# Which expert matrices are converted ahead of time, how many conversions run at once, and how four tiles are gathered: a two-layer mixer and mixture-of-experts trunk on eight cores

## The reference

```python
for l in range(DEPTH):                       # 2
    m = hybrid_mixer(x, w_in[l], ..., w_o[l])
    x = layer_norm(ALPHA * x + m, ln1_g[l], ln1_b[l])
    f = grouped_moe(x, router_w, router_b, exp_w_gate[l], exp_w_up[l], exp_w_down[l])
    x = layer_norm(ALPHA * x + f, ln2_g[l], ln2_b[l])
```

```python
for e in range(N_EXPERTS):                   # 16, width 512, two of them per token
    h = jax.nn.silu(xt @ w_gate[e]) * (xt @ w_up[e])
    y = y + dense_gates[:, e:e + 1] * (h @ w_down[e])
```

## Time and profile before

| what | value |
|---|---|
| runs | 2025.96, 2028.21, 2029.23 us; median 2028.21 |
| profiled execution, its time | 2037.57 us |
| its span on the slowest core (core 2) | 2036.5 us |
| spans of the eight cores | 2007.5 to 2036.5 us |
| TensorE, VectorE, ScalarE, GpSimd busy | 62%, 51%, 31%, 24% of the span |
| first mixer, first expert stage | to about 598 us, 598 to 961 us |
| second mixer, second expert stage | 961 to 1549 us, 1549 to 1902 us |
| last gathers, norm and stores | from 1902 us |

### The profile page before, as it was taken

One profiled execution on the slowest core, in us unless ns is written; L12 is line 12 of the kernel. 1 busy time (PEld: TensorE's weight loads), 2 busy tenths in 40 slices (PEclk: granted clock), 3 DMA queues, 4 the chain that ended last, 5 costly groups with the idle time before them and its releaser, 6 DMA issues.

```text
span 2036.5 us, 23801 instructions; the slowest of 8 cores (2007.5 to 2036.5 us)
## 1 busy us (share of the span) xinstructions
PE 1260.2 (62%) x7040; PEld 640.8 (31%) x7040; DVE 1041.5 (51%) x2328; ACT 637.1 (31%) x1109; POOL 496.1 (24%) x361
## 2 busy tenths in 40 slices
PE   0577868586429698685254687767535967878200
PEld 0433333232215454342121233333223534544000
DVE  1357486757733232232279658675761322323597
ACT  0344544435202222120254254443421211211122
POOL 4011315041340000001845112303031000000597
PEclk9897879798659899897567798978766989989655
DMA  9947667759848999997965878974124999997663
GB/s 199 260 137 99 99 94 125 104 89 180 160 123 208 260 224 249 246 236 222 206 134 64 112 93 115 125 89 90 63 84 144 236 244 230 247 256 168 225 210 131
DMA packets 78766, 334.99 MB, mean 164 GB/s; under 512 B 10776, under 2 KB 22688, under 8 KB 62880
## 3 DMA queue, kind: packets, MB, share of 16 engines
q0 software_dynamic: 26384, 166.16, 50.1%
q1 hardware_dynamic: 52240, 167.14, 25.3%
HBM read 362.71 MB, written 147.19 MB: 250 GB/s over the span
## 4 chain that ended last, share of the span: by engine, by line
PE 38%; DMA 17%; DVE 16%; issue 15%; ACT 8%; POOL 3%; DVEq 0%; SPq 0%; ACTq 0%; another core or an unknown queue 0%; POOLq 0%
PE pb L596 36%; DMA yg<-s_scr 6%; DMA s_wbuf<-ew 3%; DMA s_xy<-xg 3%; DMA s_xtok<-x 2%; ACT s_scr L605 2%; PE pT L1287 1%; ACT s_xy L641 1%; DVE s_sm L624 1%; ACT L605 1%; ACT s_xtok L605 1%; DVE s_scr L609 1%; DVE s_sm L675 1%; DVE s_scr L616 1%; DVE s_xtok L609 1%
## 5 line engine op out<-in xcount | busy, mean ns | idle before, releaser
L596 PE MATMUL pb<-s_xy,s_wbuf 128*128 128x352 bf16 (+2 forms) x2992 | 657.4, 349 | 145.2 <-ACT s_scr L605 34.5
L596 PEld LDWEIGHTS pb<-s_xy,s_wbuf 128*128 128x128 bf16 x2992 | 288.6, 104 | 396.3 <-issue 237.0
L596 PE MATMUL pb<-s_wbuf,s_scrb 128*128 128x512 bf16 (+1 forms) x768 | 232.1, 399 | 51.6 <-DMA s_wbuf<-ew 28.4
L616 DVE TENSOR_SCALAR s_scr<-pb,s_gsl 128x512 f32<-128x512 f32 (+1 forms) x192 | 135.6, 745 | 234.8 <-PE pb L596 167.6
L596 PE MATMUL pb<-s_wbuf,s_xy 128*128 128x512 bf16 x792 | 239.2, 412 | 8.9 <-DVE s_xtok L624 2.2
L609 POOL TENSOR_TENSOR s_xtok<-s_xtok,s_lnp 128x1024 f32<-128x1024 f32 x76 | 183.8, 2422 | 199.8 <-ACT s_xtok L605 153.4
L609 DVE TENSOR_TENSOR s_scrb<-s_scr,pb 128x352 bf16<-128x352 f32 x128 | 64.6, 519 | 229.9 <-PE pb L596 218.8
L406 POOL DMA_DIRECT2D s_wbuf<-exp_w x42 | 22.4, 532 | 645.8 <-PE pb L596 577.8
L641 ACT COPY s_xy<-pT 128x1024 bf16<-128x1024 bf16 (+1 forms) x96 | 90.3, 940 | 283.4 <-PE pT L1287 253.2
L1287 PE MATMUL pT<-s_identb,s_xy 128*128 128x128 bf16 (+1 forms) x768 | 121.9, 226 | 89.0 <-DMA s_xy<-xg 53.2
L709 PE MATMUL pT<-s_identb,s_scr 128*128 128x128 bf16 x336 | 55.0, 273 | 182.2 <-ACT s_scr L605 70.5
(11 more groups left out here) (119 smaller groups left out, 1619.2 us busy)
## 6 DMA issues: line engine op xcount, KB each, us to landing
ew<-exp_w POOLq DMA_DIRECT2D x36, 1536.0 KB, 17.8
s_wbuf<-ew SPq DMA_DIRECT2D x54, 1024.0 KB, 14.6
s_wbuf<-exp_w POOLq DMA_DIRECT2D x42, 1024.0 KB, 15.4
yg<-s_scr SPq DMA_DIRECT2D x64, 512.0 KB, 15.0
s_xy<-xg SPq DMA_DIRECT2D x32, 514.0 KB, 13.4
yg<-s_scr SPq DMA_DIRECT2D x32, 384.0 KB, 17.8
xg<-s_gov SPq DMA_DIRECT2D x2, 5808.0 KB, 31.4
s_xtok<-x SPq DMA_DIRECT2D x17, 512.0 KB, 10.6
```

Of the source, the lines that this page charges most:

```text
L596: em.op(PE, lambda e: e.matmul(out.ap, lhsT.ap, rhs.ap, start=start, stop=stop), w=[out], r=[lhsT, rhs])
L616: em.op(E, lambda e: e.tensor_scalar(out=out.ap, in0=a.ap, scalar1=a1, scalar2=None, op0=op0), w=[out], r=rr)
```

## The change

Three things:

1. `PRE` becomes all experts but 3, 7, 11 and 15: 12 of 16 are converted ahead, four are loaded from float32. A layer has 24 conversions of experts instead of 18, and 12 converting loads instead of 21.
2. `NTOK` becomes 3, and the planner charges a conversion 4 bytes per element instead of 6 (11.65 us at 270 GB/s instead of 17.5).
3. Between the layers tiles 0 to 3 are gathered plainly into four staging places in `wbuf` from column 16384 on, the place of w_o, and added by `vt`; tiles 2 and 3 reuse the places of 0 and 1. w_o is loaded after that, at the start of the second layer's list, and no longer before the branch. Tiles 4 to 16 are gathered as before.

```diff
-PRE = [e for e in range(NE) if e % 2 == 0 or e == 1]
+PRE = [e for e in range(NE) if e % 4 != 3]
...
-NTOK = 2
+NTOK = 3
...
                 em.dma(POOL, ewD[l].ap[e, h * 64:(h + 1) * 64, :], ew_d[l, e, h * 64:(h + 1) * 64, :], "dew%d" % k,
-                       w=[ewD[l].rows(2 * e + h, 2 * e + h + 1), tok[k].rows(0, 1)], r=after, size=64 * 12288 * 6)
+                       w=[ewD[l].rows(2 * e + h, 2 * e + h + 1), tok[k].rows(0, 1)], r=after, size=64 * 12288 * 4)
...
-                   w=[wmD.rows(h, h + 1), tok[k].rows(0, 1)], r=[gtok.rows(NT - 1, NT)], size=32 * 24576 * 6)
+                   w=[wmD.rows(h, h + 1), tok[k].rows(0, 1)], r=[gtok.rows(NT - 1, NT)], size=32 * 24576 * 4)
...
             if l > 0:
+                stg = [View(wbuf, 16384 + k * 2 * D, F32, D) for k in range(4)]
+                for i in range(4):
+                    for k in range(2):
+                        c, g = k * NT + i, stg[(2 * i + k) % 4]
+                        gc = gai(2 * i + k, 2 * i + k + 1)
+                        em.gather(g().ap, ygD[l - 1].ap, gc.ap, "dg%d" % c, w=[g(), gtok.rows(i, i + 1)],
+                                  r=[ygD[l - 1].rows(0, NSLOT + 1), gc])
+                    for k in range(2):
+                        vt(xtile(i), stg[(2 * i + k) % 4](), xtile(i), ALU.add)
+                load_layer_weights(l, only=[4])
                 for (t0, nb) in MBLOCKS:
                     for k in range(2):
-                        for i in range(t0 // 128, (t0 + nb) // 128):
+                        for i in range(max(4, t0 // 128), (t0 + nb) // 128):
                             c_gather(k, i, ygD[l - 1])
...
-                load_layer_weights(l + 1)
+                load_layer_weights(l + 1, only=range(4))
```

## The result

The changed kernel takes 2099.84 us (median of four runs) where the kernel before takes 2027.39 in the same comparison: a ratio of 1.0343, 95% interval 1.0312 to 1.0375. It is 3.4% slower; 1970 was forecast, with a range up to 2008. The ratio leaves out the fourth run, 2121.36 us, in which four of the cores showed a lower granted clock (0.77 to 0.79 in place of 0.80). The profiled execution took 2100.09 us, its span 2099.0 on core 2, the slowest again.

A forecast was written before the change was run, and what follows sets the result against it. It took full DMA to bound the expert stages and chains over four engines the mixers; -52 - 9.9 + 0 - 7 + 10.2 = -58.7 us from the 2028.2 median gives 1970 us, range 1942 to 2008.

The forecast's parts named there:

- Part 1: Expert stages: three more experts a layer read as bf16 save 26 us a stage, 52 for both; bounds 13 and 31.4.
- Part 2: End of the first layer: without the output matrix's load ahead, the last store lands sooner, gaining 9.9 us; bounds 5 and 9.9.
- Part 3: Between the layers: four plainly gathered tiles change nothing, 0 us; bounds a gain of 8, a loss of 10.
- Part 4: Mixers: more conversions planned closer make GpSimd wait and cost 10.2 us; bounds 0 and 80.
- c: Mixers: the time one conversion piece takes when others are queued, 12.6 us as the mean of four bursts.
- the half of the lateness: Mixers: of 20.4 us by which the last pieces run late, half, 10.2 us, was taken to lengthen the kernel.
- the prediction's own formulas: Lateness at a mixer's last piece, piece time against planned time: 12.1 us in the first layer, 8.3 in the second.
- E: Rival, mixers: pieces take 13.9 us and all lateness passes on, losing 80 us; +11, 2040 us; decided at 13.65; chance 0.08.
- Part 5: End of the first mixer: the last conversion no longer stands among the late scatters, gaining 7 us, between 0 and 11.7.

The follow-up runs named there:

- e1: Changed kernel, but each layer converts only expert 0 and all bf16 experts read expert 0's matrices: 1963.2 us, ratio 0.965 to the kernel before.
- e9: Changed kernel with copies of expert 0's bf16 form in place of the other eleven experts' conversions: 1971.4 us, ratio 0.971 to the kernel before.
- e11: Kernel before with w_o loaded later, ten experts converted in the first layer and twelve in the second, 14.6 us a piece, three under way: 1982.9 us, ratio 0.975.
- e13: Kernel before with w_o loaded later, twelve experts converted in both layers, 14.6 us a piece, three under way, all gathers adding: 2011.2 us, ratio 0.989.
- e14: Kernel before with w_o loaded later, eleven experts converted in the first layer and twelve in the second, 14.6 us a piece, three under way: 1991.0 us, ratio 0.980.
- e2: Kernel before with only the gathers' change: four tiles gathered plainly and w_o loaded after them: 2040.4 us, ratio 1.0035.
- e6: Kernel before with only the load of w_o moved behind gathers of the second layer, all gathers adding: 2039.2 us, ratio 1.0015.
- e5: Changed kernel with the planner's price of a conversion at 14.6 us a piece in place of 11.65: 2046.4 us, ratio 1.0047 to the kernel before.
- e10: Kernel before with only the planner's price of a conversion changed, 11.65 us in place of 17.5: 2097.9 us, ratio 1.033.

## Why the prediction was wrong

**Part 1** was right in kind and too small: the second stage is 36.9 us shorter (26 taken, 31.4 the upper bound), the first 38.2, of which part 2 has about 10. In the other runs with twelve experts (e1, e9, e11, e13, e14) the second stage gains 29 to 35 us. 31.4 counted only what the three experts' own transfers save, and was no bound. The queues in the first stage, 660 to 950 us:

```profile
q1 hardware_dynamic: 15206, 61.07, 63.9%
q0 software_dynamic: 1649, 12.07, 26.3%
```

They moved 73.1 MB in 290 us, 252 GB/s, against 238 in the earlier trace rows; the two take 90.2% in place of 96.9%. The rates held (3.03 and 6.32 us per MB, 3.05 and 6.38 taken), so the step that was short is the one from bytes saved to time saved; what else comes off is not shown.

**Part 2** held at its own place: the last store is followed by the first gather when it has landed, after 4.53 us (3 to 5 forecast; 12.9 before):

```profile
981.92 4.53 DMA yg<-s_scr
```

e2 has 10.3 us for it in the stage. What failed is that this gain would reach the end: in e6 the whole is no faster.

**Part 3** failed. The gathers came as forecast (the one right behind tile 3's second landed 60.9 us after the first gather, 63 forecast for tile 3's), and I added the 20 us of before. But the tile is not complete with the gather, it is complete with the addition, and I placed "one behind all 34 gathers" without asking what stands on VectorE ahead of the other. The block began after 112.0 us, not 83; the part cost 14 us (e2) to 27 (e5 against e13) in mixer 2, outside my bound of 10.

**Part 4** is the step that decided. Its mechanism was right; two of its terms were not: the time of a piece, c = 12.6 us, and the half of the lateness that was to reach the end, 10.2 us in all. With 14.4 us in the place of c the prediction's own formulas give 25 x 14.4 - 302.9 = 57 us in mixer 1 and 21 x 14.4 - 256.3 = 46 in mixer 2. Measured are 60.8, and 61.5 less the 14 to 27 of part 3, 35 to 48. For two under way (piece n waits for n - 2) the formula gives 43 and 32 for e10, measured 41.7 and 24.3.

That these agree so closely is partly luck. From the first to the last issue of a conversion it took 377 us in mixer 1 and 302 in mixer 2 (means of the cores), 74 and 45 more than the 302.9 and 256.3 planned: in mixer 1 a piece with its share of the scatters in the queue took 15.1 us, not 14.4, and 61 of the 74 us reached the end. In e10 the issues were 53 and 36 us late (298 and 234, planned 245 and 198), and 41.7 and 24.3 arrived. So two thirds of the lateness or more arrive; I let half of it pass, for which no row spoke.

Why 12.6? I read the ends of four bursts from shares in slices of 0.7 to 1.1 us. Those rows are mostly zeros, and yet the queue's row for the same windows shows it busy for 90.4% of 28 us and 92.1% of 44 (here for 1087.1 and 1206.1, two and three pieces; the third row is core 2 of the changed kernel, 1130 to 1370 us, full all the time):

```profile
q0 software_dynamic: 128, 3.15, 90.4%
...
q0 software_dynamic: 191, 4.72, 92.1%
```

```profile
q0 software_dynamic: 1067, 26.12, 98.5%
```

By these a piece took 12.7 and 13.5 us of the queue's time, not 11.6 and 13.9, and 14.2 when the queue stays full; the other two windows give 12.7 and 13.5 as well, a mean of 13.1. 96 of the 128 packets of the first carry the data, 32 are of under 512 B, so one takes 25.3 x 16 / 96 = 4.2 us there, six slices; the digits show where packets start, and shares in slices shorter than a packet tell nothing of an end.

Why 13.1 and then 14.2? Not because a burst is short. In the four windows core 3 was busy for 84% to 94% of the time, and a packet took 4.2 to 4.5 us; in the changed kernel both cores of a pair are busy all the time, and it takes 4.7 (the table by e9). In mixer 2 of the kernel before only 44% of the conversion packets ran beside a neighbour over 90% busy, in the changed kernel 89%. The same reading on core 0 at 1157 us would have given 7.6 us. So c was never a property of the piece: the change, which closes the gaps in every core's queue, raises it. No row of the prediction looked at the neighbour.

The rival that came true is E, by its own mechanism and past its point of decision, 13.65 us: its price of 80 us at c = 13.9 would be 103 at 14.4, and the time 2062 us; part 3 (14 to 27 us) and the wider spread of the cores (about 14 us) bring most of the rest. I gave it 0.08 because the slowest of four samples was its condition. But the change aimed at exactly the state that was measured least: the queue full all the time, on both cores of a pair.

Two neighbours with full queues move 2 x 4.72 MB, read and written, in 14.2 us, 665 GB/s. The Trainium skill, HBM Reference, Specifications (TRN2), gives a pair of cores 716 GB/s; by this rule, an estimate, a piece takes 13.2 us or more while both convert. The trace agrees with it as a floor: 14.2 us measured, 93% of that rate.

**Part 5** gave nothing. From the first late scatter (607.41) to the first transposition (660.48) it takes 53.1 us, as before (52.7). The last conversion no longer stands there, so it had cost nothing; the second layer's tail is still shorter (1607.74 to 1650.02, 42.3 us), and the s_dgm products, which only the first has, are the likely difference, with the loads beside them; neither was tried alone.

## What to carry to other kernels

A planner's price of a transfer is a promise to every engine queued behind it: set it by what the transfer takes when the queues of both cores of a pair are full, not by a burst that happens to meet an idle neighbour (7.6 against 14.2 us here). An in-order engine passes most of an underprice on, times the count (e10: one number, 3.3%). Fill a background queue only as far as the stage lasts at that rate, and look at what else is issued beside its last pieces: up to there a piece is nearly free here, beyond it it costs 8 to 13 us of its 14, mostly because one small load that the next step needs is held up beside it. And a tile is ready with the last operation on it, not with its last transfer: ask on each engine what stands ahead of that operation.

## What the runs showed of the hardware

The two cores of a pair (0 and 1, 2 and 3, 4 and 5, 6 and 7) share what a transfer from DRAM to DRAM needs, and other cores have no part in it. In mixer 2 of the kernel before (1080 to 1450 us) a conversion packet takes 2.59 us beside an idle neighbour (2548 packets) and 4.53 beside a full one (2997). Sorted in addition by any core outside the pair, it takes 2.54 to 2.81 us with the neighbour idle and, but for 4.09 in one group of 148, 4.44 to 4.66 with it full, whether that third core is idle or full.

The cores' spans lie further apart when both queues are full. In the profiled execution of the changed kernel mixer 2 takes 657.1 us on the mean of cores 0, 2, 4, 6 and 637.7 on that of 1, 3, 5, 7; before the change there is no such difference (585.5 and 586.4). It is not that odd cores are served better. From 1130 to 1370 us cores 2 and 3 both had 797 conversion packets, and the row of core 3 has more MB than core 2's above only by the rows scattered in that time:

```profile
q0 software_dynamic: 1374, 27.20, 98.9%
```

And in another run of the same kernel it is core 0 that ends first, at 2041.2 us, and core 1 at 2090.5. What parts the two cores of a pair was not found.
